# Routing from unnormed chunks, a shorter choice of experts, the branch before the weights, and a 19th load buffer

## The reference, cut to what matters

```python
h = h + memory_cross_attention(...) # ends with o @ w_xo
t = rms_norm(h, norm_moe)
g_logits = t @ w_rg + b_rg # 4 groups of experts
g_w = softmax(g_logits)[argmax(g_logits)]
e_logits = t @ w_re + b_re # 32 experts, 8 a group
e_in = e_logits of the chosen group
top_v, top_i = lax.top_k(e_in, 2)
w_top = softmax(top_v) * g_w
y = sum over the two: w_top * (silu(t @ w_gate[e]) * (t @ w_up[e])) @ w_down[e]
```

## Time and profile before

| | |
|---|---|
| three runs | 1187.24, 1188.03, 1188.97 us; median 1188.03 |
| profiled execution | 1185.96 us, span 1184.2 us, mean granted clock of PE 0.947 |
| busy in the span | PE 1040.6 us (88%), PEld 951.4, DVE 639.5 (54%), ACT 528.2 (45%), POOL 7.8 |
| HBM | 234.45 MB read, 199 GB/s over the span |
| chain that ended last | PE 61%, DVE 14%, DMA 12%, ACT 8%, issue 3% |

### The profile page before, as it was taken

One profiled execution on the slowest core, in us unless ns is written; L12 is line 12 of the kernel. 1 busy time (PEld: TensorE's weight loads), 2 busy tenths in 40 slices (PEclk: granted clock), 3 DMA queues, 4 the chain that ended last, 5 costly groups with the idle time before them and its releaser, 6 DMA issues.

```text
span 1184.2 us, 19472 instructions
## 1 busy us (share of the span) xinstructions
PE 1040.6 (88%) x8600; PEld 951.4 (80%) x8600; DVE 639.5 (54%) x822; ACT 528.2 (45%) x712; POOL 7.8 (1%) x13
## 2 busy tenths in 40 slices
PE   3999997799978989997698777679999989999998
PEld 3999885799978889987665444448999879999998
DVE  6697656765554587444311111107996556555556
ACT  4476557564654556351211011116755555444444
POOL 0000000000000000000000000000000000000000
PEclk9999998899999999998599888889999989999999
DMA  6564321143502355369079999995432315555540
GB/s 259 178 213 180 111 104 72 71 159 135 214 36 72 136 185 186 135 264 417 41 306 421 421 420 420 420 415 221 172 143 72 151 75 214 200 188 178 212 145 37
DMA packets 34247, 236.80 MB, mean 200 GB/s; under 512 B 3952, under 2 KB 4592, under 8 KB 6256
## 3 DMA queue, kind: packets, MB, share of 16 engines
q1 hardware_dynamic: 32976, 232.54, 51.3%
q0 software_dynamic: 464, 2.12, 0.5%
q10 hardware_dynamic: 720, 0.85, 0.2%
HBM read 234.45 MB, written 1.05 MB: 199 GB/s over the span
## 4 chain that ended last, share of the span: by engine, by line
PE 61%; DVE 14%; DMA 12%; ACT 8%; issue 3%; SPq 1%; DVEq 0%; ACTq 0%
PE ps L436 14%; PE ps L437 14%; PE ps L438 14%; DMA wr<-in_c_weights 7%; DVE wlo L1757 4%; DMA raw<-in_c_weights 3%; ACT whi L1180 3%; PE ps L1110 2%; DMA xlo<-in_c_weights 2%; PE ps L484 2%; SPq L2602 1%; PE ps L553 1%; PE ps L1096 1%; PE ps L858 1%; PE ps L1138 1%
## 5 line engine op out<-in xcount | busy, mean ns | idle before, releaser
L1757 DVE TENSOR_TENSOR wlo<-raw,whi 128x2048 fp32r<-128x2048 f32 (+2 forms) x123 | 274.3, 2233 | 135.1 <-ACT whi L1180 135.1
L436 PE MATMUL ps<-XUh,whi 128*128 128x256 f32 x1032 | 293.3, 284 | 14.0 <-DVE XUl L1763 7.9
L437 PE MATMUL ps<-XUl,whi 128*128 128x256 f32 x1032 | 288.8, 280 | 0.0
L438 PE MATMUL ps<-XUh,wlo 128*128 128x256 f32 x1032 | 288.6, 280 | 0.0
L1180 ACT ACTIVATE whi<-raw 128x2048 fp32r<-128x2048 f32 (+2 forms) x123 | 228.6, 1861 | 71.4 <-PE ps L438 70.6
L436 PEld LDWEIGHTS ps<-XUh,whi 128*128 128x128 f32 x1032 | 195.9, 190 | 17.4 <-issue 14.9
L437 PEld LDWEIGHTS ps<-XUl,whi 128*128 128x128 f32 x1032 | 196.1, 190 | 0.9 <-issue 0.8
L438 PEld LDWEIGHTS ps<-XUh,wlo 128*128 128x128 f32 x1032 | 196.6, 190 | 0.0
L1110 PE MATMUL ps<-wr,Xg 128*32 128x256 f32 x400 | 51.2, 457 | 21.9 <-DMA raw<-in_c_weights 12.2
L2564 DVE SCALAR_TENSOR_TENSOR sphs<-sphs,wsl,ps 128x256 f32<-128x256 f32 x8 | 3.8, 480 | 112.9 <-ACT sphs L1728 112.9
L1110 PEld LDWEIGHTS ps<-wr,Xg 128*32 128x32 f32 x400 | 25.2, 131 | 37.9 <-issue 32.9
(11 more groups left out here) (531 smaller groups left out, 2401.3 us busy)
## 6 DMA issues: line engine op xcount, KB each, us to landing
raw<-in_c_weights SPq DMA_DIRECT2D x142, 1024.0 KB, 4.9
wr<-in_c_weights SPq DMA_DIRECT2D x39, 1024.0 KB, 26.7
xhi<-in_c_weights SPq DMA_DIRECT2D x15, 1024.0 KB, 26.1
xlo<-in_c_weights SPq DMA_DIRECT2D x15, 1024.0 KB, 26.4
T<-in_c_weights SPq DMA_DIRECT2D x5, 1024.0 KB, 27.0
raw<-in_c_weights SPq DMA_DIRECT2D x4, 576.0 KB, 3.6
raw<-in_c_weights SPq DMA_DIRECT2D x3, 512.0 KB, 6.6
H<-in_c_x SPq DMA_DIRECT2D x1, 1024.0 KB, 5.6
```

The source lines that it names most:

```text
L436: pe.matmul(ps, h(k), xh(k), start=start and k == 0, stop=False, skip_group_check=loose)
L437: pe.matmul(ps, h(k), xl(k), start=False, stop=False, skip_group_check=loose)
L438: t = pe.matmul(ps, l(k), xh(k), start=False, stop=stop and k == kt - 1, skip_group_check=loose)
L1757: dve.tensor_tensor(l[:, 0:n], r, h[:, 0:n].bitcast(F32), ALU.subtract).then_inc(*did("w_lo", "split", i))
```

## The change

1. **Norm.** ACT squares each chunk of `xo` as it is added and multiplies chunks 0 to 2 by the gain into `T8b`; DVE does so for the last chunk and adds up the squares. The sum comes from four matmuls with the tokens as the stationary side, so r is a column of tokens, `rmoe`. `T8b` isn't multiplied by r any more: the logits are taken of the unnormed chunks, the first six features' tiles before the sum is there, and r goes into the bias step of the logits and into the copies to `XT`.
2. **Choice.** `first_of` takes four steps in place of five (a falling ramp and a maximum). The experts outside the chosen group are pushed down by a large negative number, and the choice is made over all 32 columns, so that the marks needn't be spread.
3. **Branch.** The count of tokens has a bank and an event of its own and comes before the ranks. PE, ACT and DVE jump behind the ranks; `Pg` of group 0 is made before DVE's jump, straight from the places. The transpose of `comb`, its spreading and `posrow` are done inside the sparse form, the first behind the gather of group 0, the second behind its gate and up. `up` waits for each half of the gathered tokens by itself.
4. **Buffers.** The 8 KB area of the routing's own small tiles becomes the 19th load buffer, `wr7`, free when the routing's last step has read them.

The diff, cut to its core:

```diff
-    stock += [("wr", 6), ("T8", 0)]
+    stock += [("wr", 6), ("T8", 0), ("wr", 7)]
...
+    spare["wr", 7] = R("wr7", [128, PIECE], F32, 16 * KB)
...
+            ("wr", 7): ("route", "free")}
...
-        w.wait_ge(*at_("n_moe", "dst", 1))
+        def logits(ks):
+            for k in ks:
+                w.wait_ge(*at_("n_moe", "x", k // 2))
+                for j in range(2):
+                    t = pe.matmul(lg_ps[:, 64 * j:64 * j + 36], T8b[:, k, 128 * j:128 * j + 128], wr[:, k, :],
+                                  start=k == j == 0, stop=k == 7, skip_group_check=True)
+            return t
+        logits(range(6))
+        ps, free = bank.take("n_moe", "ms")
+        w.wait_ge(*free)
+        w.wait_ge(*at_("n_moe", "acc"))
         for j in range(2):
-            for k in range(8):
-                t = pe.matmul(ps[:, 64 * j:64 * j + 36], T8b[:, k, 128 * j:128 * j + 128], wr[:, k, :], start=k == 0, stop=k == 7)
-        t.then_inc(*did("route_pe", "lg_ps"))
-        for j in range(2):
-            for q in range(2):
+            for h in range(2):
+                t = pe.matmul(ps[:, 4 * j:4 * j + 4], T8[:, h, 128 * j:128 * j + 128], ones[:, 0:4], start=h == 0, stop=h == 1)
+        t.then_inc(*did("norm_pe", "n_moe", "ms"))
+        logits((6, 7)).then_inc(*did("route_pe", "lg_ps"))
+        for q in range(2):
+            for j in range(2):
...
                 t.then_inc(*did("route_pe", "xtok", j, q))
+        ps, free = bank.take("count")
+        w.wait_ge(*free)
+        w.wait_ge(*at_("route", "sel"))
+        for j in range(2):
+            t = pe.matmul(ps[:, 0:32], ones[:, :], sel[:, j, :], start=j == 0, stop=j == 1)
+        t.then_inc(*did("route_pe", "count_ps"))
...
-        ps, free = bank.take("combT")
-        w.wait_ge(*free)
-        w.wait_ge(*at_("route", "comb"))
-        for j in range(2):
-            t = pe.transpose(ps[:, 128 * j:128 * j + 128], comb[:, j, :], ident)
-        t.then_inc(*did("route_pe", "combT_ps"))
...
-            w.wait_ge(*at_("emptied", *use))
+        pe.matmul(ps[:, 32:64], strict[:, :], sel[:, 1, :], start=False, stop=True).then_inc(*did("route_pe", "rank_ps"))
...
+        def turn_positions():
+            ps, free = sbank.take("combT", among=(4,))
+            w.wait_ge(*free)
+            for j in range(2):
+                t = pe.transpose(ps[:, 128 * j:128 * j + 128], comb[:, j, :], ident)
+            t.then_inc(*did("moe_pe", "moe", "combT"))
+        def spread_positions():
+            ps, free = sbank.take("posrow", among=(5,))
+            w.wait_ge(*free)
+            w.wait_ge(*at_("moe", "combT_out"))
+            for k in range(2):
+                t = pe.matmul(ps[:, 256 * k:256 * k + 256], ident[0:64, 32 + k:33 + k].broadcast_to([64, 128]), combT[0:64, :])
+            t.then_inc(*did("moe_pe", "moe", "posrow"))
...
-            w.wait_ge(*at_("emptied", "gx", g, 1))
...
+                    w.wait_ge(*at_("emptied", "gx", g, k // 4))
...
+        turn_positions()
...
+            if g == 0:
+                spread_positions()
+                yb = [sbank.take("sy", j, among=(4 + j,)) for j in range(4)]
...
-        side = norm("n_moe", H, 8, 1024, col["norm_moe"], ("emptied", "xo", 3), [("n_xattn", "lo", 1)])
-        finish(side)
...
+            w.wait_ge(*at_("n_xattn", "lo", 1))
+            w.wait_ge(*at_("emptied", "xo", c))
+            square("n_moe", T8, H[:, 2 * c:2 * c + 2, :], c)
+            if c < 3:
+                for k in (2 * c, 2 * c + 1):
+                    t = copy(T8b[:, k, :], H[:, k, :], scale=col["norm_moe"][:, k:k + 1])
+                t.then_inc(*did("norm_act", "n_moe", "x", c))
+        table(LOGEXP)
+        w.wait_ge(*at_("n_moe", "ms"))
...
+        act.activation(rmoe, sums, ACT.Ln, scale=1.0 / 1024, bias=epsc).then_inc(*bank.emptied("n_moe", "ms"))
+        w.wait_ge(*at_("emptied", "n_moe", "ms"))
+        act.activation(rmoe, rmoe, ACT.Exp, scale=-0.5).then_inc(*did("norm_act", "n_moe", "r"))
+        w.wait_ge(*at_("n_moe", "r"))
...
-                copy(XT[:, j, 512 * q:512 * q + 512], bank.ps("xtok", j, q)[:, :]).then_inc(*bank.emptied("xtok", j, q))
+                copy(XT[:, j, 512 * q:512 * q + 512], bank.ps("xtok", j, q)[:, :], scale=rmoe[:, j:j + 1]).then_inc(*bank.emptied("xtok", j, q))
...
-        w.wait_ge(*at_("posrow_ps"))
-        copy(posrow[:, :, :], halves(bank.ps("posrow"))).then_inc(*bank.emptied("posrow"))
...
+        gather(0)
+        w.wait_ge(*at_("moe", "combT"))
+        copy(combT[:, :], sbank.ps("combT")[:, 0:256]).then_inc(*sbank.emptied("combT"))
+        marks.value["moe", "combT_out"] = marks.value["emptied", "combT"]
         table(SILU)
-        gather(0)
...
+            if g == 0:
...
+                copy(posrow[:, :, :], halves(sbank.ps("posrow"))).then_inc(*sbank.emptied("posrow"))
...
         for c in range(4):
             upcoming("xo", c)
             residual("xo", c)
-        finish(norm("n_moe", H, 8, 1024, col["norm_moe"], T8b, ("emptied", "xo", 3), []))
+            if c == 3:
+                w.wait_ge(*at_("emptied", "xo", 3))
+                dve.tensor_tensor(T8b[:, 6:8, :], H[:, 6:8, :], col["norm_moe"][:, 6:8].unsqueeze(2).broadcast_to([128, 2, 256]),
+                                  ALU.mult).then_inc(*did("norm_dve", "n_moe", "x", 3))
+            if c:
+                w.wait_ge(*at_("n_moe", "sq", 0))
...
-        def first_of(dst, v, mx_, n, s):
-            r_(dve.tensor_tensor(dst, v, mx_.unsqueeze(2).broadcast_to([128, 2, n]), ALU.is_equal))
-            r_(dve.tensor_scalar(s, dst, -1000.0, 1000.0, ALU.mult, ALU.add))
-            r_(dve.tensor_tensor(s, s, iota[:, 0:n].unsqueeze(1).broadcast_to([128, 2, n]), ALU.add))
-            r_(dve.tensor_reduce(rt[:, 254:256], s, AX.X, ALU.min))
-            r_(dve.tensor_tensor(dst, iota[:, 0:n].unsqueeze(1).broadcast_to([128, 2, n]), rt[:, 254:256].unsqueeze(2).broadcast_to([128, 2, n]), ALU.is_equal))
+        def first_of(dst, v, mx_, n, s, op=ALU.is_equal):
+            r_(dve.tensor_tensor(s, v, wide(mx_, n), ALU.is_equal))
+            r_(dve.tensor_tensor(s, s, falling[:, 0:n].unsqueeze(1).broadcast_to([128, 2, n]), ALU.mult))
+            r_(dve.tensor_reduce(top, s, AX.X, ALU.max))
+            r_(dve.tensor_tensor(dst, s, wide(top, n), op))
...
-        dve.memset(comb[:, :, :], 0.0)
-        w.wait_ge(*at_("xa_pT", 1, 1))
-        dve.tensor_tensor(strict[:, :], ones[:, :], tri, ALU.subtract)
+        w.wait_ge(*at_("n_moe", "r"))
+        for j in range(2):
+            t = dve.scalar_tensor_tensor(out=lg[:, j, 0:36], in0=bank.ps("lg")[:, 64 * j:64 * j + 36], scalar=rmoe[:, j:j + 1],
+                                         in1=brt[:, 0:36], op0=ALU.mult, op1=ALU.add)
+        t.then_inc(*bank.emptied("lg"))
...
-        first_of(og, gl, gm, 4, s4)
-        r_(dve.tensor_tensor(big, el.rearrange("p j (g e) -> p j g e", g=4), og.unsqueeze(3).broadcast_to([128, 2, 4, 8]), ALU.mult))
-        r_(dve.tensor_reduce(ein, big.rearrange("p j g e -> p j e g"), AX.X, ALU.add))
-        r_(dve.tensor_reduce(m1, ein, AX.X, ALU.max))
-        first_of(o1, ein, m1, 8, s8)
-        r_(dve.scalar_tensor_tensor(out=ea, in0=o1, scalar=-3.0e38, in1=ein, op0=ALU.mult, op1=ALU.add))
+        first_of(ng, gl, gm, 4, s4, op=ALU.not_equal)
+        r_(dve.scalar_tensor_tensor(out=elm.rearrange("p j (g e) -> p j g e", g=4), in0=ng.unsqueeze(3).broadcast_to([128, 2, 4, 8]),
+                                    scalar=-3.0e38, in1=el.rearrange("p j (g e) -> p j g e", g=4), op0=ALU.mult, op1=ALU.add))
+        r_(dve.tensor_reduce(m1, elm, AX.X, ALU.max))
+        first_of(ohs[:, :, 0, :], elm, m1, 32, s32)
+        r_(dve.scalar_tensor_tensor(out=ea, in0=ohs[:, :, 0, :], scalar=-3.0e38, in1=elm, op0=ALU.mult, op1=ALU.add))
         r_(dve.tensor_reduce(m2, ea, AX.X, ALU.max))
-        first_of(o2, ea, m2, 8, s8)
         dve.tensor_tensor(dl, m2, m1, ALU.subtract).then_inc(*did("route_dve", "route", "dl"))
-        for k, o in enumerate((o1, o2)):
-            r_(dve.tensor_tensor(ohs[:, :, k, :].rearrange("p j (g e) -> p j g e", g=4), o.unsqueeze(2).broadcast_to([128, 2, 4, 8]),
-                                 og.unsqueeze(3).broadcast_to([128, 2, 4, 8]), ALU.mult))
+        first_of(ohs[:, :, 1, :], ea, m2, 32, s32)
         dve.tensor_tensor(sel[:, :, :], ohs[:, :, 0, :], ohs[:, :, 1, :], ALU.add).then_inc(*did("route_dve", "route", "sel"))
...
+        w.wait_ge(*at_("count_ps"))
+        dve.tensor_reduce(rt[:, 253:254], bank.ps("count")[:, 0:32], AX.X, ALU.max).then_inc(*bank.emptied("count"))
+        w.wait_ge(*at_("emptied", "count"))
+        dve.tensor_copy(flag[:, 0:1], rt[:, 253:254]).then_inc(*did("route_dve", "route", "flag"))
+        dve.reciprocal(gw, gs).then_inc(*did("route_dve"))
+        w.wait_ge(*at_("rank_ps"))
...
+        r_(dve.tensor_tensor(place2[:, :, :, :], ohs[:, :, :, :], rk[:, :, 0:32].unsqueeze(2).broadcast_to([128, 2, 2, 32]), ALU.mult))
```

(8 more changed lines are left out.)

134 lines of the change are left out of this document (71 added, 63 removed).

## The result

The changed kernel took **1172.43 us** (median of 4 runs, 1167.95 to 1173.78) against 1187.63 for the kernel before in the same session (median of 4, 1184.14 to 1188.97): ratio 0.986, 95% interval 0.9835 to 0.9885. The forecast was 1167.9 with a range of 1164.0 to 1174.5. The time lies inside the range and 4.5 us above the forecast; the gain is 15.2 us where 20.1 were forecast. A second session gave 1170.81 (6 runs), ratio 0.984 (0.9809 to 0.9871). Over both, the changed kernel has a mean of 1171.1 in 10 runs; the kernel before has 1188.8 over the 35 runs of all sessions: 17.7 us. The profiled execution of the changed kernel took 1173.18, with a span of 1171.4; the one before took 1185.96, with 1184.2.

The account below looks back on a forecast made before the run. Bound: the experts' load stream, started by the first buffer release behind the routing's chain of small steps. Gains 19.2 (release) + 2.5 (buffer) - 1.6 (late load) = 20.1 us; 1188.0 - 20.1 = 1167.9 us, range 1164.0 to 1174.5.

Parts of the forecast that it names:

- Logits: Norm and logits behind xo: first 24 matmuls at full clock, 2.9 us; logits at DVE at 556.9, gain 11.8.
- the rival: In the logits: the clock falls to half as soon as xo ends, +3.6 us, 1171.5; chance 0.10.
- Choice and flag: In the routing: choice takes 5.0 us, marks at 561.9; count comes first, flag 1.6 behind at 563.5.
- Jump: PE's jump from flag to gather: 4.2 us as in the kernel before, ending at 567.7.
- a cheap jump: Before gate: the 4.2 us weren't the jump, or the gather has full clock; 1.3 to 2.8 us better; chance 0.08.
- The fetch meets the stream: At PE's jump: the page's fetch waits behind the first loads, 2.5 to 3.7 us, 1171.0; chance 0.10.
- First group: Experts' group 0: gather 6.5, slots 0.9, transpose 0.7, together 8.1 us; release 3.68 after gate and up start.
- The stretch and the buffer: Experts' loads: their end follows the release one for one; the 19th buffer saves one piece, 2.5 us.
- the stretch would not follow: Experts' loads: DMAs run dry once or PE's late steps bound; half the gain goes, 1178; chance 0.06.
- a change that does nothing: Experts' loads don't start earlier, as something behind the jump is late by all of it; chance 0.02.
- The second block's first load: Start of the second block: hz 0's load waits for the last down, 1.6 us lost, between 1.0 and 2.3.
- The slower ending: Second block stays one load late, 56 pieces each 0.43 us late: 24 us lost, 1190.4; chance 0.02.

Follow-up runs that it names:

- the wide logits: Changed kernel with the logits' and norm sum's matmuls written over 108 and 128 columns instead of 36 and 4: 1167.3 us, ratio 0.9836.
- the kernel with the middle join: Changed kernel with PE's gathering body first, cut in two by the dense body (groups 0 to 3, then 4 to 7): 1171.66 us, ratio 0.986.
- the turned order: Changed kernel with the ring of 19 load buffers beginning with wr3 in place of the first raw buffer: 1166.12 us, in a later session 1167.99.

## Why the prediction was right, and by how much it was off

**The path to the release.** The sum of the steps gave 27.05 us from the last residual to the release; measured were 26.35 and 26.96. That the sum comes out is luck in part: the logits (0.4 to 1.2 us) and the jump (0.9 to 2.1) were too cheap, the first group (2.1 to 2.3) and the flag (0.4) too dear, and these errors offset each other:

| step | forecast | profile 1 | profile 2 |
|---|---|---|---|
| residual to logits at DVE | 4.45 | 5.67 | 4.89 |
| logits to marks standing | 5.0 | 4.91 | 4.91 |
| marks to flag | 1.6 | 1.22 | 1.23 |
| flag to gather | 4.2 | 5.09 | 6.26 |
| gather to gate | 8.1 | 5.8 | 6.0 |
| gate to release | 3.7 | 3.7 | 3.7 |

- *Logits.* "I take the full clock" was right for the first 24 matmuls (2.76 us against 2.9) and wrong for the rest: the sum and the last eight took 1.47 and 1.90 us at the half clock. The clock did not fall as soon as `xo` ended, as the rival had it, but 2.8 and 3.7 us behind the last residual. Of that rival's 3.6 us, 0.4 to 1.2 came true. In six of the twelve profiles with the change, two of them wide, the logits stood within 4.5 us.
- *Choice and flag.* As forecast within 0.5.
- *Jump.* This is the term that was mis-sized: 4.2 forecast, 5.09 and 6.26 measured (4.75 to 6.72 in all seven profiles that read the flag and jump right behind it). What it was read from is right: in the kernel before PE waits for `posrow` (to 582.60), reads the flag at 582.74 for 0.49 us, and then stands 3.34 us in its compare-and-branch. That instruction in the first profile of before, the changed kernel's first and second, and the wide logits:

```profile
L806 PEldq COMPARE_BRANCH  x1: 3335/3335/3335, 583.3 to 583.3; - x1
L813 PEldq COMPARE_BRANCH  x1: 3802/3802/3802, 566.6 to 566.6; - x1
L813 PEldq COMPARE_BRANCH  x1: 5042/5042/5042, 563.5 to 563.5; - x1
L814 PEldq COMPARE_BRANCH  x1: 5502/5502/5502, 561.5 to 561.5; - x1
```

  The step that failed is "I take 4.2 for the jump, now from the flag": it carries over a jump made with idle DMAs to a place where the first loads are still landing. With the two bodies exchanged the branch at the gather takes 0.09 us, so it is the jump and not the emptied bank, and the rival "a cheap jump" falls, in so far as the jump goes. By the Trainium skill (Advanced Engine Details and Errata, Control Flow Timing) a compare-and-branch takes about 108 ns; the trace agrees for branches that stay in order (0.07 to 0.09 us) and not for those over the dense body (3.34 us at the least). Another 0.4 us of the excess is the changed code's own: PE's waits for the emptied banks stood ahead of the flag before and now stand behind the jump, four semaphore instructions from 570.6 to 571.0.
- *The fetch meets the stream.* Borne out, at a lower price than the 2.5 to 3.7 it was given. From the start of the branch to its instruction packet it was 0.95 and 0.92 us in the kernel before's two profiles, where the DMAs were idle. In the seven profiles it was 1.1 to 3.0, and the packet moved when the loads had just landed or were nearly through. Stretches of the wide logits, whose packet moved at 564.52, 2.98 us behind the branch's start (the last number but one is the DMAs' share):

```profile
561.50:562.50 1.00, 0.00 (x0) 0.00 (x0) 0.91 (x4) 0.00 (x0) 0.00 (x0) 0.50 1.00 418
562.50:563.50 1.00, 0.00 (x0) 0.00 (x0) 0.93 (x5) 0.00 (x0) 0.00 (x0) 0.50 1.02 426
563.50:564.50 1.00, 0.00 (x0) 0.00 (x0) 0.86 (x6) 0.00 (x0) 0.00 (x0) 0.50 0.70 287
564.50:565.50 1.00, 0.00 (x0) 0.00 (x0) 0.23 (x2) 0.00 (x0) 0.00 (x0) 0.50 0.12 41
```

  From the packet to the end of the branch it was 2.4 to 2.8 us, with idle DMAs and with busy ones. So the forecast's argument against this rival, a share of 0.20 by 565 to 567 in the kernel before, did not carry over: in the changed kernel's first profile the share was 1.01 over 562 to 567. Against 0.95 before, the packet came 0.35 us later there and 1.6 later in the second profile. Two jumps in the middle of the full stream, at the join and ahead of group 4, had their packets 4.1 and 3.5 us behind the start of the branch. There PE still ran its own matmuls until 0.4 and 0.8 us before the packet, so these two do not tell whether the packet waited for the loads or for PE. DMA queues from 661 to 664 us in the kernel with the middle join:

```profile
q1 hardware_dynamic: 163, 1.20, 97.0%
q8 instruction: 1, 0.02, 2.1%
```

  That a jump out of the loaded pages waits for a DMA (Runtime: NRT & Kernel Launch, Instruction fetch mechanics, of the Trainium skill) agrees with the packet that moved in each of them.
- *First group.* The gather at 6.5, as with the half clock before, was too dear: the clock was 0.80 over 572 to 577, and 32 matmuls took 5.24. The gather's better clock was priced in the range at 2.8 and came to 1.3, and 1.0 came from what stands around it. The forecast itself counted on none of that clock; over the twelve profiles its 32 matmuls took 5.2 to 6.4 us.

**The stretch and the buffer.** 197.1 instead of 199.2: 2.1 us for 2.5 forecast. That the stretch would not follow is out; so is a change that does nothing.

**The second block's first load.** 1.6 forecast, with bounds of 1.0 and 2.3; the split came 2.76 and 1.41 later. The mechanism is as forecast, down to the chain: last `down`, SP's issue, the load. The second piece took 8.46 us in the first profile and 7.10 in the second, against 4.7 + 2.5 and up to 1.2 more. What the forecast had at nothing is SP's issue: the load starts 4.15 us behind the start of the last `down` in both profiles, where 3.67 was reckoned. With it the first profile's loss lies above the upper bound. The slower ending, with 56 late pieces, did not come: from the split to the end it was 381.2 and 379.6 us against 379.7 in the kernel before at the same pace, and 380.9 and 381.3 in the turned order, where no load is late.

**What is left.** With the two second profiles the terms add up: 1.3 (ahead of the routing, chance) + 18.6 + 2.0 - 1.4 + 0.1 = 20.6, the difference of their spans. With the first pair it is -1.7 + 19.9 + 2.2 - 2.8 - 4.8 = 12.8. The 17.7 of the 45 runs lie between them. The path, the stretch and the load were each good to 1.2 us. Of the 4.5 us from forecast to median, 2.1 are which executions were drawn: the mean of the changed kernel's ten runs lies 1.3 below that median, and the mean of the kernel before's 35 lies 0.8 above the 1188.0 that the forecast started from. The other 2.4 stay (20.1 forecast, 17.7 measured, with a standard error of 0.8). The buffer's and the load's terms together were 0.3 to 1.5 too kind (0.9 forecast, -0.6 and 0.6 measured). About 1.5 of the 2.4 I can't assign. From the split to the end, eleven profiles with the change took 380.9 on average (379.5 to 381.8), the one profile of the kernel before with their pace 379.7; with one profile that stays open.

## What to carry to other kernels

- Where a branch's usual body stands behind a long rare one, each run pays the jump; put the usual body first and place the jump where the engine waits anyway. Here that was 3 us of path for an exchange of two blocks. A duration read at one place of the program, such as the jump's 4.2 us, holds for what the DMAs did there.
- Look at the branch instruction itself, and not only at the idle time of the engine behind it: its start, its length and the instruction packet inside it tell a wait for data, the reading of the flag and the fetch apart.
- A buffer more in a turning list also turns who follows whom: check which buffer the first load of the next stage inherits, and reorder the list so that it is one that comes free early.
- Cut two profiles at common events before you compare their spans, and profile both kernels twice; 3.3 us of the difference between the first two spans here lay in a stretch that no edit touches.

## What the hardware showed beyond that

- The same matmuls at granted clock 1.00, with PE busy throughout, ran at 871 or 851 per 100 us in two executions of one kernel. The start of the last residual lay between 549.96 and 558.86 us in the twelve profiles of the changed kernel and its variants, and at 550.81 and 558.08 in two of one kernel, which ran on two chips.
- The clock fell from 2.4 to 1.2 GHz in the middle of uninterrupted work, 2.7 to 4.3 us after the last residual in seven of the twelve profiles, and in the other five not for 9 us. Of the six with the logits within 4.5 us, four had it down in the count and the ranks and began the one-hot matrix 13.2 to 13.3 us behind the residual; the other two did so at 12.2 and 12.3. Without such logits it was 12.4 to 13.6.
- A compare-and-branch of PE took 0.07 to 0.09 us where it went on in order, 3.34 and 3.71 where it jumped over the dense body with idle DMAs, 3.54 to 5.50 with the first loads or `wr7`'s still landing (eight profiles), and 6.1 to 6.4 in the full stream of loads (four). In these last four PE's idle time was only 2.97 to 3.99 us, as matmuls already in its queue ran on beside the branch.
- In all fourteen, 2.4 to 2.8 us pass from the instruction packet to the end of the branch.
